# Pairing experts of different groups in the expert stage of a two-layer trunk

## What is computed

```python
_, grp = lax.top_k(g_logits, 1)                       # one group of four
e_in = jnp.take_along_axis(e_logits, grp[:, :, None], axis=1)[:, 0]
top_val, top_idx = lax.top_k(e_in, MOE_TOP_K)         # two experts of that group
gates = jax.nn.softmax(top_val, axis=-1) * g_w
expert = grp * MOE_EXPERTS_PER_GROUP + top_idx
...
y = (jax.nn.silu(rows @ w_gate[e]) * (rows @ w_up[e])) @ w_down[e]
return y * wts[:, None]
...
out = jax.ops.segment_sum(ys.reshape(R, D), row_tok, num_segments=T + 1)[:T]
```

## Time and profile before

| | |
|---|---|
| median of 3 runs | 2276.2 us (2276.02 to 2276.87) |
| profiled execution | 2278.48 us |
| its span, first to last instruction | 2276.7 us |
| expert stage of layer 0, first to last scatter | 687.54 to 1002.30 us |
| expert stage of layer 1, first to last scatter | 1956.90 to 2267.61 us |
| scatters, both layers | 36 with `moe_index`, 28 with `moe_half_index` |
| gathers, both layers | 50 |
| busy share of the span | PE 88%, DVE 42%, ACT 31%, POOL 20% |

### The profile page before, as it was taken

The page is one execution under the profiler, slowest core; times in us unless marked ns, Lnnn a source line. Parts: engine busy times, 40 slices in busy tenths (PEclk is TensorE's granted clock), DMA queues, the critical chain, the costliest instruction groups (busy, mean ns, idle before and its releaser), DMA issues. The chain is left out here.

```text
span 2276.7 us, 30320 instructions
## 1 busy us (share of the span) xinstructions
PE 2001.5 (88%) x11289; PEld 1276.3 (56%) x11289; DVE 946.1 (42%) x2302; ACT 697.5 (31%) x1761; POOL 465.0 (20%) x609
## 2 busy tenths in 40 slices
PE   6999859999979989848999768999999997999785
PEld 3444436655577645634655535666666556776453
DVE  3996774533341111104223486666664225111111
ACT  4013555531101111103122576666764110111110
POOL 0001003321012222110000254454543001122221
PEclk9999869999979999979999878999999997999898
DMA  5000010121489999726000100001001118799992
GB/s 213 0 0 0 0 47 20 38 87 75 177 353 327 393 363 369 290 61 210 1 0 1 77 1 11 11 11 47 20 11 56 60 74 347 274 382 395 353 363 57
DMA packets 82905, 317.23 MB, mean 139 GB/s; under 512 B 18064, under 2 KB 23207, under 8 KB 65862
## 3 DMA queue, kind: packets, MB, share of 16 engines
q1 hardware_dynamic: 66342, 272.23, 30.6%
q0 software_dynamic: 16416, 43.03, 7.1%
HBM read 276.75 MB, written 55.23 MB: 146 GB/s over the span
## 5 line engine op out<-in xcount | busy, mean ns | idle before, releaser
L1681 PEld LDWEIGHTS experts_gu_ps<-experts_x_cols,moew_w 128*128 128x128 f32 x2048 | 236.4, 195 | 15.7 <-issue 15.7
L1681 PE MATMUL experts_gu_ps<-experts_x_cols,moew_w 128*128 128x128 f32 x2048 | 240.1, 279 | 4.6 <-DVE experts_x_cols L1767 4.6
L1108 POOL TENSOR_SCALAR nsaatt_probs<-nsaatt_probs,nsaatt_inv,trunk_gates_or_logits 128x384 f32<-128x384 f32 (+7 forms) x256 | 186.4, 743 | 200.9 <-DVE nsaatt_inv L1135 200.9
L1844 DVE TENSOR_SCALAR trunk_x_rows<-experts_y_ps,experts_gates 128x512 f32<-128x512 f32 x50 | 37.6, 751 | 325.7 <-DMA x_kept<-trunk_x_rows,moe_half_index 87.8
L1079 ACT ACTIVATE nsaatt_probs<-nsaatt_probs,nsaatt_bias 128x384 f32<-128x384 f32 (+7 forms) x256 | 169.0, 667 | 8.5 <-DVE nsaatt_bias L1130 8.5
L1037 PE MATMUL nsaatt_turn<-trunk_ident,nsaatt_probs 128*128 128x128 f32 x912 | 124.2, 279 | 23.8 <-DVE nsaatt_probs_cols L1001 9.5
L1027 PE MATMUL nsaatt_scores<-layer_k_cols,trunk_x_rows 64*128 64x384 f32 (+3 forms) x640 | 129.6, 516 | 14.7 <-DVE nsaatt_top L1121 13.5
L1783 ACT ACTIVATE trunk_x_rows<-experts_y_ps,experts_gates 128x512 f32<-128x512 f32 x50 | 34.4, 687 | 349.4 <-DMA x_kept<-trunk_x_rows,moe_half_index 86.8
L1083 ACT ACTIVATE nsaatt_probs_cols<-nsaatt_turn 128x512 f32<-128x512 f32 (+1 forms) x204 | 96.5, 514 | 118.8 <-PE nsaatt_turn L1037 117.5
L1037 PEld LDWEIGHTS nsaatt_turn<-trunk_ident,nsaatt_probs 128*128 128x128 f32 x912 | 97.6, 141 | 58.1 <-issue 37.3
L1723 PE MATMUL experts_y_ps<-moew_w,experts_hid 128*128 128x512 f32 x256 | 115.3, 593 | 2.0 <-DVE trunk_x_rows L1844 2.0
(11 more groups left out here) (418 smaller groups left out, 3527.2 us busy)
## 6 DMA issues: line engine op xcount, KB each, us to landing
moew_w<-in_moe_w_gate_dram SPq DMA_DIRECT2D x54, 1024.0 KB
moew_w<-in_moe_w_up_dram SPq DMA_DIRECT2D x54, 1024.0 KB
moew_w<-in_moe_w_down_dram SPq DMA_DIRECT2D x54, 1024.0 KB
trunk_x_rows<-in_moe_w_gate_dram SPq DMA_DIRECT2D x10, 1024.0 KB
trunk_x_rows<-in_moe_w_up_dram SPq DMA_DIRECT2D x10, 1024.0 KB
trunk_x_rows<-in_moe_w_down_dram SPq DMA_DIRECT2D x10, 1024.0 KB
trunk_x_rows<-in_x_dram SPq DMA_DIRECT2D x16, 512.0 KB, 8.0
h_rows<-out_h_rows SPq DMA_DIRECT2D x16, 512.0 KB, 2.6
```

Of the source, the lines that this page charges most:

```text
L1108: pool.tensor_scalar(part(s, r, h), part(s, r, h), inv[:, s % BUFS, i:i + 1], 1.0 if gate is None else gate[h], ALU.mult, ALU.mult).then_i ...
L1681: last = pe.matmul(to, wm[:, c, half * P:(half + 1) * P], x_cols[:, b, c, :], start=(c == 0), stop=(c == CHUNKS - 1))
```

## The change

1. `FIXED` is the number of groups: the first expert of each group (0, 8, 16, 24) has a kept place, 0 to 3, and SP asks for all four before the routing is known. At most seven experts of a group can then be narrow.
2. The 14 narrow experts are numbered by expert number instead of by count (`nth`), and number k shares a block with number k + 7. Partners are thus of different groups, and no token is in both.
3. A pair is scattered once, with `index`; `half_index` and `no_half` are gone, and the waits on `y_sent` count units.
4. DVE copies a pair's turned hidden values ahead of the weighing of the unit before.
5. Up to 18 extra blocks, in groups of 6.

```diff
-FIXED = 2
+FIXED = GROUPS
...
-MORE_BLOCKS = 16
-MORE_GROUP = 8
+MORE_BLOCKS = 18
+MORE_GROUP = 6
...
-                for e in range(FIXED):
-                    count_off(tie[:, e:e + 1], [[1, 1]], 2 * (FIXED - e) * SEQ * EXPERTS)
-                count_off(tie[:, FIXED:], [[-1, EXPERTS - FIXED]], EXPERTS - 1 - FIXED)
+                for g in range(GROUPS):
+                    first = g * PER_GROUP
+                    count_off(tie[:, first:first + 1], [[1, 1]], 2 * (GROUPS - g) * SEQ * EXPERTS)
+                    count_off(tie[:, first + 1:first + PER_GROUP], [[-1, PER_GROUP - 1]], EXPERTS - 2 - first)
...
-                mine.link(dve.tensor_scalar(no_half[:, 0:1], part_no[:, :], float(CAP), float(SEQ), ALU.is_ge, ALU.mult))
-                mine.link(dve.tensor_scalar(no_half[:, 1:2], part_no[:, :], float(CAP), float(SEQ), ALU.is_lt, ALU.mult))
-                mine.link(dve.tensor_tensor(no_half[:, :], no_half[:, :], over(no_token[:, :], (P, 2)), ALU.add))
...
+                mine.link(dve.tensor_scalar(narrow[:, :], place[:, :], float(WIDE), None, ALU.is_ge))
+                mine.link(dve.tensor_tensor_scan(nth[:, :], ones[:, 0:EXPERTS], narrow[:, :], 0.0, ALU.mult, ALU.add))
+                mine.link(dve.tensor_scalar(second[:, :], nth[:, :], float(HALF_NARROW + 1), float(2 * HALF_NARROW - 1), ALU.is_ge, ALU.mult))
+                mine.link(dve.scalar_tensor_tensor(out=nth[:, :], in0=nth[:, :], scalar=2.0, in1=second[:, :],
+                                                   op0=ALU.mult, op1=ALU.subtract))
+                mine.link(dve.scalar_tensor_tensor(out=nth[:, :], in0=nth[:, :], scalar=float(WIDE - 2), in1=place[:, :],
+                                                   op0=ALU.add, op1=ALU.subtract))
+                mine.link(dve.tensor_tensor(nth[:, :], nth[:, :], narrow[:, :], ALU.mult))
+                mine.link(dve.tensor_tensor(place[:, :], place[:, :], nth[:, :], ALU.add))
...
-                mine.link(dve.tensor_scalar(cap[:, :], place[:, :], float(WIDE), float(CAP - P), ALU.is_ge, ALU.mult))
-                mine.link(dve.tensor_scalar(cap[:, :], cap[:, :], float(P), None, ALU.add))
+                mine.link(dve.tensor_scalar(cap[:, :], narrow[:, :], float(CAP - P), float(P), ALU.mult, ALU.add))
...
-                for half in range(2):
-                    dve.tensor_scalar(half_index[:, half, :], index_ps[:, WIDE:UNITS], no_half[:, half:half + 1], None, ALU.add)
...
-                        pool.wait_ge(y_sent, 16 * FIRST_LOAD[n])
+                        pool.wait_ge(y_sent, 16 * n)
...
-                    if paired(n):
-                        add_to_tokens(n % 2, half_index[:, 0, u - WIDE:u - WIDE + 1])
-                        pool.wait_ge(y_sent, 16 * (FIRST_LOAD[n] + 1))
-                        add_to_tokens(n % 2, half_index[:, 1, u - WIDE:u - WIDE + 1])
-                    else:
-                        add_to_tokens(n % 2, index[:, u:u + 1])
+                    add_to_tokens(n % 2, index[:, u:u + 1])
...
+                    if n + 1 < UNITS and paired(n + 1):
+                        take_hidden(n + 1)
                     if n == 0:
                         dve.wait_ge(gates_ready, 1)
                     if n >= 2:
-                        dve.wait_ge(y_sent, 16 * FIRST_LOAD[n - 1])
+                        dve.wait_ge(y_sent, 16 * (n - 1))
                     weigh_y(n, n % 2, gates[:, u:u + 1])
-                    if n + 1 < UNITS and paired(n + 1):
-                        take_hidden(n + 1)
...
-                load_expert(nc.sync, A, layer, s, w[s], w_here[s])
+                load_expert(nc.sync, A, layer, s * PER_GROUP, w[s], w_here[s])
```

More of the change, by code:

```diff
@@ L1287, in spin, with route @@
         pe.transpose(spare[:, 0:P], ident[:, :], ident[:, :])
-def route(nc, name, logits, ident, ones, index, half_index, order, order_ready, row_hot, block_hot, parts, ratio, extra_end, turn_no,
+def route(nc, name, logits, ident, ones, index, order, order_ready, row_hot, block_hot, parts, ratio, extra_end, turn_no,
           loads):
@@ L1298, in route @@
         HALF_TILES = T // 2
+        HALF_NARROW = NARROW // 2
         not_before = ph.sb("not_before", [P, P])
@@ L1306, in route @@
         place = ph.sb("place", [P, EXPERTS])
+        narrow = ph.sb("narrow", [P, EXPERTS])
+        nth = ph.sb("nth", [P, EXPERTS])
+        second = ph.sb("second", [P, EXPERTS])
         cap = ph.sb("cap", [P, EXPERTS])
@@ L1337, in route @@
         no_token = ph.sb("no_token", [P, 1])
-        no_half = ph.sb("no_half", [P, 2])
         spare = ph.ps("spare")
@@ L1344, in route @@
             "made", "carry_made", "own", "exps_ready", "summed", "ranked", "token_hot", "row_hot", "indexed"))
-        MADE = 12 + FIXED
+        MADE = 11 + 2 * GROUPS
         with nc.Block() as block:
@@ L1504, in _, with experts @@
                 dve.tensor_scalar(index[:, :], index_ps[:, 0:BLOCKS], no_token[:, 0:1], None, ALU.add)
-                for half in range(2):
-                    dve.tensor_scalar(half_index[:, half, :], index_ps[:, WIDE:UNITS], no_half[:, half:half + 1], None, ALU.add)
-def experts(nc, name, layer, w, w_here, ident, ones, index, half_index, order, order_ready, more, row_hot, block_hot, parts, ratio,
+def experts(nc, name, layer, w, w_here, ident, ones, index, order, order_ready, more, row_hot, block_hot, parts, ratio,
             extra_end, turn_no, h_dram, x_kept, y, pool_sems, A):
@@ L1531, in experts @@
         more_f = ph.sb("more_f", [1, MORE_BLOCKS + 1])
-        over_group = ph.sb("over_group", [1, 1])
+        over_groups = ph.sb("over_groups", [1, MORE_BLOCKS // MORE_GROUP])
         own, gate_hot_ready, more_ready = ph.sem("own"), ph.sem("gate_hot"), ph.sem("more")
@@ L1796, in _ @@
                     if n >= 2:
-                        act.wait_ge(y_sent, 16 * FIRST_LOAD[n - 1])
+                        act.wait_ge(y_sent, 16 * (n - 1))
                     weigh_y(n, n % 2, gates[:, u:u + 1])
@@ L1803, in extra @@
                     sigmoid(n, 0)
-                    act.wait_ge(y_sent, j * 16 + 16 * EXPERTS)
+                    act.wait_ge(y_sent, j * 16 + 16 * UNITS)
                     act.wait_ge(column_ready, j * 2 + 2)
@@ L1863, in weigh_rows @@
                     size = float(MORE_GROUP)
-                    mine.link(dve.tensor_scalar(over_group[:, :], total, size, size, ALU.is_gt, ALU.mult))
-                    mine.link(dve.tensor_scalar(more_f[:, MORE_BLOCKS:], total, 0.0, size, ALU.is_gt, ALU.mult))
-                    mine.link(dve.tensor_tensor(more_f[:, MORE_BLOCKS:], more_f[:, MORE_BLOCKS:], over_group[:, :], ALU.add))
+                    for i in range(MORE_BLOCKS // MORE_GROUP):
+                        mine.link(dve.tensor_scalar(over_groups[:, i:i + 1], total, i * size, size, ALU.is_gt, ALU.mult))
+                    mine.link(dve.tensor_reduce(more_f[:, MORE_BLOCKS:], over_groups[:, :], X_AXIS, ALU.add))
                     dve.tensor_copy(more[:, :], more_f[:, :]).then_inc(more_ready, 1)
@@ L1892, in extra @@
                     hidden_wide(n, 0)
-                    dve.wait_ge(y_sent, j * 16 + 16 * EXPERTS)
+                    dve.wait_ge(y_sent, j * 16 + 16 * UNITS)
                     dve.wait_ge(column_ready, j * 2 + 2)
@@ L1902, in wait_for_results @@
 def wait_for_results(pool, used, y_sent, whole):
-    pool.wait_ge(y_sent, used * 16 + 16 * EXPERTS)
+    pool.wait_ge(y_sent, used * 16 + 16 * UNITS)
     pool.sem_inc(whole, 1)
@@ L2067, in moe @@
         index = ph.sb("index", [P, BLOCKS], I32)
-        half_index = ph.sb("half_index", [P, 2, UNITS - WIDE], I32)
         order = ph.sb("order", [P, 1], I32)
@@ L2085, in loads @@
                     load_place(sp, A, layer, i, order, w, w_here)
-            route(nc, f"route{layer}", logits, ident, ones, index, half_index, order, order_ready, row_hot, block_hot, parts, ratio,
+            route(nc, f"route{layer}", logits, ident, ones, index, order, order_ready, row_hot, block_hot, parts, ratio,
                   extra_end, turn_no, loads)
-            return experts(nc, f"experts{layer}", layer, w, w_here, ident, ones, index, half_index, order, order_ready, more, row_hot,
+            return experts(nc, f"experts{layer}", layer, w, w_here, ident, ones, index, order, order_ready, more, row_hot,
                            block_hot, parts, ratio, extra_end, turn_no, h_dram, x_kept, y, pool_sems, A)
```

2 lines of the change are left out of this document (1 added, 1 removed).

## The result

The changed kernel takes 2250.4 us (median of 4 runs, 2250.39 to 2251.68) against 2276.1 us before (2275.32 to 2276.87): a ratio of 0.9889, 95% interval 0.9871 to 0.9906. It is faster by 25.7 us. The forecast was 50 us faster, 2226 us with a range up to 2248, so half of the expected gain is missing, and the time lies 2 us outside the range. The profiled execution's span is 2248.7 us.

The account below looks back on a forecast made before the run. Scatters were taken to set the end, with DMA nearly full. PE's floor, delayed by weights, gave gains of 24.8 us (layer 1) and 28.0 (layer 0), less 1.5 a layer for slow clock: 49.8, so 2226 us, range 2202 to 2248.

Parts of the forecast that it names:

- What bounds the kernel: Both expert stages: one scatter after another sets the end, with the DMA engines having next to nothing in reserve behind.
- the floor by PE: Expert stages with DMA keeping up and PE never held: 75 us gained in all, 2201 us; chance 0.2 as a rival.
- The beat of 11.63 us: Expert stages: time a unit takes between two weighings where nothing stalls.
- Part 1: Expert stages: one scatter for a pair removes 71 us of chain a layer; a pair's scatter takes 11.2 us.
- The rival that a pair's landing grows with its rows: Expert stages: scatters stay the bound, a pair landing after say 16 us; 2251 us, chance 0.12.
- The Trainium skill's fit: GpSimd DMAs: 2.0 us fixed plus bytes over 436 GB/s; merging all 14 pairs saves 28 us, 2248.
- Part 2: Expert stages: turned rows copied ahead of the weighing; 20.8 us of PE's idling goes in layer 1, 42.1 in both.
- Part 3: Before the order is known: four kept experts asked for early, 6.3 MB; nothing gained or lost.
- Part 4: Ahead of the first gather: the longer placing on DVE adds 1.0 us, say 1.1, a layer.
- Part 5: Extra blocks: none runs, as the largest narrow expert has 60 and 62 tokens of the 64 that fit.
- The weights take some back: Expert stages: at 388 GB/s the last pair's weights come late, holding PE 10.8 us in layer 1, 11.1 in layer 0.
- slow clock: Expert stages: 1.5 us a layer taken off the gain for PE's slow clock after a wait for weights.

Follow-up runs that it names:

- the four runs: Copy put back behind the weighing: changed kernel 2252.6 us, without down loads 2201.1, with earlier requests 2222.0; copy moved ahead alone in the kernel before: 2275.3.

## Why the prediction was half right

- **What bounds the kernel, and the floor: right.** The floor by PE gave 2201; with TensorE never held the runs show 2199.7. The beat of 11.63 us held.
- **Part 1: right.** 25 scatters a layer, 11 to 12 us apart where nothing holds TensorE. Behind each pair in layer 1 POOL waited for the weighing, not for the landing, so no pair's landing reached the beat of some 11.6 us to the next scatter. That fits the 11.2 taken; the landings themselves are not in the trace. The rival that a pair's landing grows with its rows is out, though its 2251 met the time by chance. The Trainium skill's fit (DMA: Bandwidth & Descriptors, "Anatomy of one DMA"), by which merging saves some 2 us (2248), met it by chance as well: the chain did shrink as the rows said, and the time was given back elsewhere.
- **Part 2: wrong in its own account, harmless in the sum.** I credited it with 42 us of TensorE's idling, and wrote that the copy "no longer stands behind a wait for a scatter". Part 1 had taken that wait away already. I took the 42 us for a cost of the copy's place, where they were a cost of the two scatters. The sum went by the floor and so did not count it twice, but the four runs show that the part could be left out.
- **Part 3: right**, nothing gained or lost.
- **Part 4: its 1.1 us is not to be seen.** The first scatter of layer 0 came 1.5 us earlier than before, not 1.1 later; over the runs it lies between 684.9 and 688.1 us, so a microsecond can't be read there.
- **Part 5: right**, no extra block ran.
- **"The weights take some back": the step that failed.** I took the landing of the last pair's weights as bytes over rate and got 241.7 us from first scatter to start of the last pair (2199.7 - 1956.9 - 1.1). It was 255.2, and the 13.5 us missed here, 14.4 in layer 0, less the 1.5 us a layer that the sum had set aside for slow clock, are the 24 us by which the gain falls short. TensorE's own account of them is short. The floor is 2187.8 - 1956.9 = 230.9 us; waits of 18.3 us and 5.1 us of slow clock make 254.3. In layer 0 waits of 20.2 and 4.5 us of slow clock make 255.6, and 256.5 were measured. The forecast had waits of 10.8 and 11.1 us.

  In the sum's own terms, 0.6 MB of my 92.2 had moved before the first scatter; the other 91.6 at 241.7 us is 379 GB/s, against 94.2 MB at 369: 2.6 MB are 6.9 us, the rate is 6.6. The trace's count for the stretch puts the surplus on SyncE's queue, with 77.5 MB (the second figure) where the 24 experts that were waited for make 75.5:

```profile
q1 hardware_dynamic: 13757, 77.50, 75.2%
```

  So bytes of later experts were moved before the last one that the pair needed. The rate of 388 GB/s after 2000 was too high: over 1984.5 to 2184.5 the changed kernel has 379, which the rows had for the whole stretch before and which I put down to TensorE's stalls. But the form of the sum was at fault, not only its numbers. It had TensorE held once, at the end. A hold comes whenever one request takes longer than its allowance of 21.8 us, and that is so from unit 10 on (waits of 1.8, 7.3, 0.7, 7.9, 0.7 us in layer 1).
- **Slow clock: too small.** 1.5 us a layer were taken; 9.46 and 9.83 instead of 7.09 make 5.1 in layer 1. By the account above they are part of the 13.5 us; whether a quicker pair would only have waited longer for the next load, no run shows.
- **The Trainium skill on HBM's limit.** The Trainium skill (DMA: Bandwidth & Descriptors, "Where 436 GB/s comes from") has 358 GB/s as binding for transfers between HBM and SBUF. The stretches here, of one core alone, show 369 to 375 over 240 us and more, scatters and gathers included, so it does not bind here either.

What stays open: why the landings of one pair are 29 us and of the next 22. That a held TensorE asks for less, and the queue then drains, fits the alternation of long and short waits, but no run isolated it. Nor do the runs say why the rate stays near 370 with the engines at a share of 1.0.

## What to carry to other kernels

When a chain that paces a stage is cut, look at what each request of the next resource still has: the time from the event that frees its buffer to the instruction that needs it, at the new pace, against its measured time from issue to landing in a full queue. Total bytes over rate can come out nearly even while single requests are 8 us late. Then look at what an instruction waits for and does not need (here the down matrix ahead of gate and up) and at how early each part of a buffer comes free; the first alone brought 6 us, the second alone nothing, both together 28. And before crediting an edit with a wait that it removes, ask whether another edit of the same change removes it too.

## What the runs showed of the hardware

- The three matrices of a load, 1 MB each and asked for one behind the other, landed in steps. Median times from issue in the changed kernel:

```profile
moew_w<-in_moe_w_gate_dram SPq DMA_DIRECT2D x54, 1024.0 KB, 14.8
moew_w<-in_moe_w_up_dram SPq DMA_DIRECT2D x54, 1024.0 KB, 20.3
moew_w<-in_moe_w_down_dram SPq DMA_DIRECT2D x54, 1024.0 KB, 24.2
```

- With one buffer fewer, and so fewer loads asked for ahead, the third of them has 15.5 us, at a rate of 359 instead of 369 GB/s from the first scatter to the last pair of layer 1. More depth bought 3% of rate and 9 us of delay.
- A chain of scatters was only 4 to 5% quicker with a third of the weight bytes left out: one every 9.6 us instead of 10.1. Behind the last weights a scatter does land sooner, after 6.69 and 4.74 us.
- A request on SyncE took 0.33 us in some places and up to 6.58 us in others (in the kernel with earlier requests), and the requests behind it on SyncE had to wait for it.
- After waits of 3.04, 3.47 and 3.57 us (the changed kernel, the one with pairs earlier, the one with five buffers) the next pair ran at the full clock (7.09 us). After one of 3.49 us it took 9.75, after one of 2.92 us 8.76 and after one of 2.59 us (the kernel with only the earlier request) 8.78. The length of the wait alone does not tell which.
